# One more input tile by token halves at five handovers, one silu later, the scan's squares one chunk later

## The reference, cut to what matters

```
for l in range(2):
    h = swiglu_ffn(rms_norm(x, ffn1_norm_pre[l]), ffn1_w_in[l], ffn1_w_out[l])   # 1024 -> 2 x 2816 -> 1024
    x = x + 0.5 * rms_norm(h, ffn1_norm_post[l])
    h = rms_norm(x, mix_norm_pre[l]) @ mix_w_in[l]
    o_gdn = gated_deltanet_group(h, ...)     # 4 heads, chunk-wise scan with a 128 x 128 state per head
    o_cm = conformer_conv_group(h, ...)      # 31-tap causal depthwise convolution, layer norm, silu
    x = x + rms_norm(concat([o_gdn, o_cm]) @ mix_w_out[l], mix_norm_post[l])
    h = swiglu_ffn(rms_norm(x, ffn2_norm_pre[l]), ffn2_w_in[l], ffn2_w_out[l])
    x = x + 0.5 * rms_norm(h, ffn2_norm_post[l])
    x = rms_norm(x, block_norm[l])

swiglu_ffn:  h = x @ w_in; gate, up = h[..., :2816], h[..., 2816:]; return (silu(gate) * up) @ w_out
scan, per chunk:  v_new = u_c - w_c S;  o = q_d S + qk v_new;  S = S * e^g + k_d^T v_new
after the scan:   o = o * rsqrt(mean(o*o) + eps) * out_g * silu(z)
```

## Time and profile before

| what | value |
|---|---|
| median of 3 runs | 1975.64 us (1975.39 to 1976.35) |
| the profiled execution, its own time | 1976.71 us |
| its span, first to last instruction | 1975.0 us |
| PE busy | 1946.8 us, 99% of the span |
| DVE busy | 1430.2 us, 72% |
| ACT busy | 1161.8 us, 59% |
| chain that ended last, by engine | PE 78%, DVE 15%, ACT 3% |

### The profile page before, as it was taken

One profiled execution on the slowest core, in us unless ns is written; L12 is line 12 of the kernel. 1 busy time (PEld: TensorE's weight loads), 2 busy tenths in 40 slices (PEclk: granted clock), 3 DMA queues, 4 the chain that ended last, 5 costly groups with the idle time before them and its releaser, 6 DMA issues.

```text
span 1975.0 us, 33173 instructions
## 1 busy us (share of the span) xinstructions
PE 1946.8 (99%) x12162; PEld 1746.6 (88%) x12162; DVE 1430.2 (72%) x2109; ACT 1161.8 (59%) x1957; POOL 149.4 (8%) x196
## 2 busy tenths in 40 slices
PE   9999999999999999999999999999999999999997
PEld 7999988878988899988889999888889888999886
DVE  5889832699885888872388888337998868888524
ACT  6576742457866667662266767325587656676513
POOL 1111000011000011100001110000110000111000
PEclk9999999999999999999999999999999999999999
DMA  6466533276222366643326664432761224666421
GB/s 177 116 153 155 144 110 102 68 170 147 65 54 86 86 150 159 156 127 96 102 65 138 156 155 121 116 103 75 171 141 45 61 78 114 153 158 148 150 96 43
DMA packets 351426, 232.52 MB, mean 118 GB/s; under 512 B 11122, under 2 KB 324948, under 8 KB 351316
## 3 DMA queue, kind: packets, MB, share of 16 engines
q1 hardware_dynamic: 327396, 177.55, 31.5%
q0 software_dynamic: 23904, 53.49, 15.0%
q10 hardware_dynamic: 16, 0.00, 0.0%
HBM read 175.43 MB, written 2.10 MB: 90 GB/s over the span
## 4 chain that ended last, share of the span: by engine, by line
PE 78%; DVE 15%; ACT 3%; issue 2%; DMA 1%; SPq 0%; POOL 0%; DVEq 0%; ACTq 0%
PE res L658 10%; PE res L660 9%; PE res L659 9%; PE res L893 8%; PE res L896 7%; PE res L895 7%; DVE u L2522 6%; PE sp L824 3%; PE sp L896 3%; PE sp L895 3%; PE sp L893 3%; PE res L824 2%; DVE cacc L2604 2%; PE sp L658 1%; PE res L755 1%
## 5 line engine op out<-in xcount | busy, mean ns | idle before, releaser
L2099 DVE TENSOR_TENSOR wl<-raw,wh 128x1024 fp32r<-128x1024 f32 (+1 forms) x167 | 197.3, 1185 | 335.2 <-ACT wh L1365 334.6
L1365 ACT ACTIVATE wh<-raw 128x1024 fp32r<-128x1024 f32 (+1 forms) x205 | 209.7, 1029 | 329.5 <-PE res L660 235.9
L893 PE MATMUL res<-xh,wh 128*128 128x256 f32 x768 | 218.1, 284 | 3.3 <-ACT wh L1523 1.7
L895 PE MATMUL res<-xl,wh 128*128 128x256 f32 x768 | 217.3, 283 | 0.0
L896 PE MATMUL res<-xh,wl 128*128 128x256 f32 x768 | 217.3, 283 | 0.0
L658 PE MATMUL res<-xh,wh 128*128 128x512 f32 x536 | 213.5, 398 | 2.1 <-DVE xl L2217 1.8
L660 PE MATMUL res<-xh,wl 128*128 128x512 f32 x536 | 208.9, 390 | 0.0
L659 PE MATMUL res<-xl,wh 128*128 128x512 f32 x536 | 208.9, 390 | 0.0
L660 PE MATMUL res<-hh,wl 128*128 128x512 f32 (+1 forms) x528 | 198.4, 376 | 0.0
L659 PE MATMUL res<-hl,wh 128*128 128x512 f32 (+1 forms) x528 | 198.4, 376 | 0.0
L658 PE MATMUL res<-hh,wh 128*128 128x512 f32 (+1 forms) x528 | 198.4, 376 | 0.0
(11 more groups left out here) (421 smaller groups left out, 4891.3 us busy)
## 6 DMA issues: line engine op xcount, KB each, us to landing
raw<-in_ffn_w_in SPq DMA_DIRECT2D x176, 512.0 KB, 4.0
wl<-raw POOLq DMA_DIRECT2D x128, 256.0 KB, 5.3
raw<-in_mix_w_in SPq DMA_DIRECT2D x48, 512.0 KB, 3.9
raw<-in_ffn_w_out SPq DMA_DIRECT2D x46, 512.0 KB, 3.9
raw<-in_ffn_w_out SPq DMA_DIRECT2D x48, 448.0 KB, 3.8
wl<-raw POOLq DMA_DIRECT2D x38, 512.0 KB, 4.6
raw<-in_mix_w_out SPq DMA_DIRECT2D x16, 512.0 KB, 4.0
xin<-in_x SPq DMA_DIRECT2D x8, 256.0 KB, 5.0
```

The source lines that it names most:

```text
L893: pe.matmul(bank, wh[:, slot, j, :], hi[:, k, :], start=first and k == 0, stop=False, skip_group_check=True)
L895: pe.matmul(bank, wh[:, slot, j, :], lo[:, k, :], start=False, stop=False, skip_group_check=True)
L1365: act.activation(wh[:, slot, 0:nk, :], raw[:, slot, 0:nk, :], ACT.Copy).then_inc(hi_full, 1)
L2099: dve.tensor_tensor(wl[:, slot, 0:nk, :], raw[:, slot, 0:nk, :], wh[:, slot, 0:nk, :].bitcast(F32), ALU.subtract).then_inc(lo_full, 1)
```

## The change

Four edits in three groups:

- `HALVED` goes from 3 to 4. Tile 3 is now worked by halves too, on ACT (`input_half(3, 0)` after `input_half(2, 0)`), on DVE (`update_half(3, 0)` and `low_half(3, 0)` between `low_half(2, 0)` and the second halves) and on PE (loops over `HALVED`). On ACT `high(u0 + 3)` then stands behind tile 4 and no longer behind tile 3.
- In ACT's first Strassen body the silu of pair 4 stands behind the four form copies of s = 1.
- In the scan `o_square(c)` moves from the end of chunk c to behind the `vn` and `Wy` copies of chunk c + 1; the last one stands after the loop.

```diff
-        HALVED = 3
+        HALVED = 4
@@ ACT, inputs
                     input_half(2, 0)
+                    input_half(3, 0)
                     for k in range(HALVED):
                         input_half(k, 1)
@@ ACT, ffn, body
                     first_part(s, odd)
-                    if first:
-                        silu(SP0 - 1, 0)
                     if final:
                         ...
                     else:
                         first_forms(s + 1, 1 - odd)
+                    if first:
+                        silu(SP0 - 1, 0)
@@ ACT, scan, for c in range(NC)
                     if c == NC - 2:
                         keys_out(c + 1)
+                    if c:
+                        o_square(c - 1)
                     if c == 0:
                         z_refill(0)
                         ...
                         act.activation(warm[:], eps[:], ACT.Sqrt)
-                    o_square(c)
+                o_square(NC - 1)
@@ DVE, next_inputs
                 low_half(1, 0, stage, gain, l)
                 low_half(2, 0, stage, gain, l)
+                update_half(3, 0, before, bl)
+                low_half(3, 0, stage, gain, l)
                 dve.wait_ge(bc_full, rows_before(bl, 2 * before + 1) + 1)
```

## The result

| | before | after |
|---|---|---|
| median of the runs | 1975.64 us (19 runs, 1974.52 to 1978.02) | 1979.75 us (19 runs, 1978.14 to 1983.96) |
| ratio, 95% interval | | 1.0022 [1.0015, 1.0029] |
| span of the profiled execution | 1975.0 us | 1980.6 us |
| PE, DVE, ACT busy | 1946.8, 1430.2, 1161.8 us | 1950.4, 1431.8, 1163.0 us |

The change makes the kernel 4.1 us slower, 3.0 to 5.7 by the interval. That lies in the range (1974.8 to 1980.3), 2 us above the forecast. The medians differ by just more than the bound of 0.2% (3.95 us), and the bound lies inside the interval, so on which side of it the change falls is not settled.

The account below looks back on a forecast made before the run. PE, busy 99% of the span, was taken as the bound. Handovers +4.75, scan -1.9 and silu -0.75 sum to +2.1 us, laid on the median 1975.64 for 1977.7 us, with 8 in 10 between 1974.8 and 1980.3.

Parts of the forecast that it names:

- PE has no slack, waits are what moves: Whole kernel: PE is busy 99% of the span, so only a pause or more work for PE moves the end.
- Handovers, +4.75: Five handovers with four tiles halved: PE loses 0.95 us at each, bounds 0.3 to 1.3 each.
- The fixed cost per DVE instruction: DVE in the handovers: three more instructions cost 0.47 by the skill's rule, 0.42 by the trace's intervals, per handover.
- Scan, -1.9: Scan chunk 2, squares one chunk later: PE's L1256 comes earlier, 0.95 us gained in each of two layers.
- Silu, -0.75: Second Strassen pair, start of `p4`: FFN 1 -0.4, FFN 2 +0.6, FFN 3 -1.05, FFN 4 +0.1; bounds -3.0 and +1.5.
- the DMA is 0.5 earlier: FFN 1: POOL's DMA comes 0.5 earlier, 0.1 of it goes at `p4`, leaving -0.4.
- 0.8 goes at `p4`, whose DVE step is where it was: FFN 3: PE is 1.5 to 1.8 earlier, then loses 0.8 at `p4` to DVE's unmoved step, leaving -1.05.
- a bound (+1.5): Silu's upper bound: POOL's DMA, beside a 512 KB weight load, lands no earlier, while `p4` waits in three FFNs.
- DVE's delay passed on in full: Rival, handovers: each costs DVE's 1.07 plus restarts, deciding from 1.32 us each; 1980.5 at 1.5 each; chance 0.16.
- the handovers do not gain: Denies the rival that tile 3's first half covers PE's wait, saving 0.5 per handover: 1969.7 us; chance 0.10.
- nothing cancelled itself: Denies the rival that silu and scan only move waits and handovers cost little over 0.3 each: 1976.6; chance 0.12.
- within 0.2%: Whole time: the outcome class of no difference beyond 0.2%, given 0.71, beside faster 0.10 and slower 0.19.

Follow-up runs that it names:

- the later remainder: Kernel before with four tiles halved, tile 3's first remainder on DVE behind the update of tile 0's second half: 1980.90 us, +4.9 (+3.2 to +6.7) against before.
- S: Kernel before with only the silu of pair 4 moved behind the form copies: 1977.08 us, +0.8 (-0.8 to +2.6) against before.
- Q + S: The change with HALVED back at 3, so squares later and silu behind the forms: 1974.67 us, -1.8 (-3.6 to +0.2) against before.
- with DVE's product later: Kernel before with the silu behind the forms and DVE's product of pair 4 behind s = 0's last remainder: 1976.13 us, 0.0 (-1.8 to +2.0).
- H: Kernel before with only the fourth halved tile (HALVED 3 to 4): 1984.12 us, +6.9 (+4.9 to +8.9) against before.
- two tiles halved: Kernel before with HALVED at 2 instead of 3, nothing else changed: 1978.92 us, +3.6 (+1.8 to +5.3) against before.
- Q: Kernel before with only the scan's squares moved one chunk later: 1973.89 us, -2.8 (-4.5 to -1.0) against before.
- the change again: The changed kernel once more, letter for letter: 1981.13 us, +4.1 (+2.4 to +5.9) against before.

## Why the prediction was right or wrong

- *PE has no slack, waits are what moves.* Right: where a handover's last product came 1.00 later, the rest of the program did, and where the scan gave 1.1, it stayed.
- *Handovers, +4.75.* Right: +5.03 and +5.06, 1.0 each for 0.95. Of the replay every step is in the trace: the wait of 0.33 kept, a new one of 0.52 in its row (0.79 less 0.16 was expected, 0.63), tile 0's second half 1.87 later (1.85), DVE's second halves from 371.88 on (371.86), fifteen waits with 7.0 us (7.5), DVE 1.05 late at the end (1.07). The 0.65 of standing still was right too, 0.66 by starts; only the sign that was named for it, an idle of 0.65 in the row, reads 0.58, since a row's idle is counted from the end that the row before gives. PE made up little of DVE's lag (0.99 to 1.06 of 1.03 to 1.05), so the replay's own sum, 0.99, was nearer than the 0.95 taken.
- *The fixed cost per DVE instruction.* Of the 1.0 per handover 0.40 to 0.42 is the price of three more instructions on as many columns; the later remainder took away 0.48 of the 0.66 of standing still. The price is the part that the Trainium skill, page "VectorE: DVE Perf Modes", section "The TRN2 errata", speaks of: by its formula for an fp32 add it would be 0.47, an estimate for all three instructions. The trace agrees with it to within 0.1.
- *Scan, -1.9.* Right: -2.13, the forecast's 0.2 given back at the column sums included (0.18).
- *Silu, -0.75.* This step failed in size: the two traces of the change have +0.38 and -0.12 for it, S alone -0.37, Q + S -0.15. FFN 2 (+0.6 forecast, +0.61 to +0.62 in all four traces) was right, and for the reason given: with DVE's product later it is -0.14. FFN 4 (+0.1, +0.09 to +0.11) was right by luck: the 0.8 to be won at the start of s = 1 was not won by the silu. S alone starts it 0.02 earlier and Q + S 0.10 later; the change's 0.72 earlier is there in H (0.65) and with two tiles halved (0.63) too, which have no silu edit. FFN 1 had "the DMA is 0.5 earlier": POOL's issue was (75.48 - 2.21 = 73.27 for 73.79), but in the first trace PE's product came at 81.38 - 2.21 = 79.17, not before the 78.86 of before, so 5.9 us behind the issue and not 5.1. The other three traces have it 0.07 to 0.27 earlier, and kernels without the edit scatter as much, so no gain can be told there. FFN 3 failed at "0.8 goes at `p4`, whose DVE step is where it was": PE was 1.78 earlier at s = 1 in all four traces and 0.63 to 0.82 earlier at `p4`, so 0.96 to 1.15 was lost where 0.8 was forecast. It was lost not to DVE but to POOL's transfer, one product ahead of `p4`, whose packets moved only as those of the load ran out, and taking DVE out of the way changed nothing. I had counted the transfers at the time of their issue; what landed with them I had only in a bound (+1.5), where the weight load was named.
- *The rivals.* DVE's delay passed on in full is what happened in kind (0.99 to 1.06 of DVE's 1.03 to 1.05), but from 1.32 each on it was to decide, and no trace has that. The two others fell: the handovers do not gain, and nothing cancelled itself.
- *The sum.* From the stretches that the edits touch the change is 5.03 - 2.13 + 0.38 = +3.3 in its first trace and 5.06 - 2.14 - 0.12 = +2.8 in its second, for +2.1. The median moved by 4.1 (3.0 to 5.7). Of these 3.3 is inside the interval and 2.8 just below it. But all the kernels with a changed handover read higher in whole runs than in the ledger of the handovers (H 6.9 for 5.2, its late remainder 4.9 for 2.7, two halved 3.6 for 2.2), while those without lie on both sides (Q -2.8 for -2.1, Q + S -1.8 for -2.3). A part of it is in TensorE's clock: each run on record has its mean granted clock, to three digits, and (1 - clock) times the span is on average 5.9 us in the runs of two halved for 4.1 in those of before beside them, 1.8 more. For H it is 0.9 more and for its late remainder 1.2 more, both with a scatter that just reaches nought; for the change again it is 0.4 less. So the clock covers the excess of two halved and perhaps half of the next two, and not that of the change. The rest, and why these runs have the lower clock, stays open.
- *The chances.* 0.71 stood on "within 0.2%", and the medians differ by 4.11 us where the bound is 3.95, so it hung on 0.16 us. With the silu at 0 the sum would have been 2.85, and "slower" would have had to be near a third.

## What to carry to other kernels

Splitting a tile to feed a waiting engine earlier pays only while the engine that does the splitting has idle time to give: here DVE needs 0.42 us more per split tile, and starts 0.66 late where a split's second step follows its first without other work between them; replay its list instruction by instruction, and try the neighbours on both sides. Moving an issue earlier is not moving a transfer earlier: look at what else is issued in the same two microseconds, and count from landing. And where several edits of one to five microseconds come together, take them apart: a gain of 2 us and a nought were hidden here by a loss of 5.

## What the runs showed of the hardware

**A late start costs twice.** In after's trace the clock fell in the start-up: from 12 to 16 us the mean granted clock is 0.63, and read by single us it is 0.53, 0.50 and 0.50 from 13 to 16, the lower of the two levels of 1.2 and 2.4 GHz. It fell behind an idle of PE of 2.56 us ahead of L658. The kernel with S and DVE's product later has the same drop behind an idle of 2.41; the eleven other traces have idles of 0.49 to 1.76 there (1.75 in before, 0.49 in the change's second trace) and no drop. Stretches of 4 us (us, busy time and count of PE, PEld, DVE, ACT, POOL; PE's clock, DMA share, GB/s), of after and of the change again:

```profile
12.00:16.00 4.00, 3.76 (x15) 3.26 (x16) 3.27 (x6) 2.15 (x4) 0.00 (x0) 0.63 1.13 277
16.00:20.00 4.00, 4.00 (x22) 3.43 (x21) 2.76 (x4) 2.68 (x5) 0.00 (x0) 0.94 0.19 34
```

```profile
12.00:16.00 4.00, 4.00 (x28) 3.48 (x27) 4.00 (x7) 2.42 (x4) 0.00 (x0) 1.00 1.15 279
16.00:20.00 4.00, 3.77 (x17) 2.78 (x17) 2.30 (x3) 3.86 (x6) 0.00 (x0) 1.00 0.18 40
```

L658 started 0.56 later than in before, because the first weights did; the drop made 2.2 of it. (1 - 0.63) and (1 - 0.94) of 4 us each are 1.7. The kernel with DVE's product later is 1.66 us late at the first Strassen pair.

**A second drop, in a busy stretch.** Eight of the thirteen traces lose 1.60 to 1.65 us between the third handover and FFN 3, the others lose nothing. Those eight, and no other, have one drop of the granted clock to the lower level there; it begins 13.0 to 14.1 us behind the handover's end each time, with PE busy 3.74 or 3.75 of the 4 us ahead of it. It comes with and without the handovers changed, and it is not a matter of the kernel alone: of the change's two traces, the same kernel, the first is without it and the second has it. The change again, and Q + S, which has none:

```profile
1016.00:1020.00 4.00, 3.75 (x23) 3.06 (x22) 2.59 (x6) 3.62 (x6) 0.00 (x0) 0.88 0.18 53
1020.00:1024.00 4.00, 4.00 (x14) 3.14 (x13) 1.99 (x4) 3.45 (x7) 0.00 (x0) 0.70 0.42 121
```

```profile
1016.00:1020.00 4.00, 4.00 (x19) 3.22 (x19) 1.98 (x6) 4.00 (x8) 0.00 (x0) 1.00 0.46 131
1020.00:1024.00 4.00, 4.00 (x23) 3.41 (x22) 3.12 (x4) 3.79 (x5) 0.00 (x0) 1.00 0.44 131
```

(0.12 + 0.30) of 4 us is 1.7; by single us the clock is 0.51, 0.50, 0.50 and 0.79 from 1019 to 1023. What sets it off is not known; it is as large as the effects under study, so one trace against one other is read by stretches and never by its span.

**A transfer's time hangs on what is issued with it.** The accumulating DMA of 256 KB was used 3.9 us or less behind its issue where the 512 KB load was issued 2.8 ahead of it, 4.0 where 1.7 ahead, and 5.8 to 5.9 where 0.2 ahead. In the last case its packets began 3.7 us behind its issue, as those of the load ended: for 1.2 us ahead of that the load's packets were the only ones.
